# Second block's input projection: value units ahead of the gate units, chunk states beside the gate units, gate chains behind the states

## The chip, the cores and the metric

One NeuronCore of a Trainium2 chip runs the whole program. The metric is device time in microseconds of one execution; three runs of the kernel before gave 2759.41, 2761.75 and 2762.43 us, median 2761.75.

## The reference

Two transformer blocks on 512 tokens of width 1024, all in float32. The first has a SwiGLU, a mixer of 16 heads and another SwiGLU. The second puts 16 learned tokens in front (528 in all), normalises, and multiplies by one input matrix of 2000 columns. Its columns are, in this order: queries q and keys k of a gated linear attention (4 heads, 64 wide each), its values v (4 heads of 128 columns), its gate r (4 heads of 128), a 16-wide decay input, and the latents of a second attention (256 for queries, 128 for keys and values, 64 for the rotated key). What matters here, cut short:

```
z = u @ w_in
q, k, v, r, a_low, q_lat, kv_lat, k_rope = split(z)
b = cumsum(log_sigmoid(a_low @ w_a2 + b_a) / 16)   per chunk of 64 tokens
att = tril((q*exp(b)) @ (k*exp(-b)).T)             within a chunk
upd = (k*exp(b_last - b)).T @ v                    one per chunk
state = exp(b_last) * state + upd                  a scan over the chunks
o = att @ v + (q*exp(b)) @ state_before
y_gla = rmsnorm(o) * gain * silu(r)
y_mla = softmax attention over the latents, with rotated queries and keys
h = h + [y_gla, y_mla] @ w_out
```

After it comes a mixture of 64 experts (2 per token) and a last norm.

## The kernel before, in words

Each engine has its own program, written out in order by hand; semaphores join them. Nothing is planned by a scheduler, so an instruction runs when all ahead of it on its engine have been issued and its own waits are met.

Weights come through six SBUF slots of 2 MB. The SP queue issues the loads in a fixed order; before each it waits until the slot is free, a signal of TensorE. The input matrix of the second block comes as four items: item 3 (latents and decay input) in slot 2, item 0 (q and k) in slot 3, item 2 (gate) in slot 4, item 1 (values) in slot 5. The loads of those two slots that follow are the two halves of the output matrix, L619.

The projection is a list of units, `UNITS`, numbered in the order in which TensorE does them. Unit n writes PSUM bank 0 (even n) or 2 (odd n), and starts when the copy of unit n − 2 to SBUF is done (`unit`, L968). Each is 8 contraction steps with 512 columns. The gate units (U_GR, four of them, one per head) and the value units (U_GV: one for the 16 learned tokens and four for 128 tokens each) are at the end of the list. Copies are done by VectorE for the units in `ON_DVE`, which holds gate units 1 and 3 of four, and by ScalarE for the others.

TensorE's order from L1076: decay input and latents, keys, queries, the turned decayed keys (`turn_keys`), four gate units, then the value units with the chunk updates 0 to 6 between them. `chunk_update(n)` (L1024) writes banks 4 to 7 in turn; it waits for the copy of its value tile and, from n = 4 on, for the state n − 3. Then come the first score product (`gla_scores(0)`, bank 0, L1031), update 7, and the first two latent units (`mla_unit`, L1065 and L1067; the second one waits for the last state). Then, for each of four heads: the output product (`gla_out`, L1045 and L1048, which waits for the masked scores and, for head 0, for the last state), the next score product, a latent unit for keys (L1072), the sum of squares (`gla_sum`, L1054) and the next two latent units.

VectorE's order: copies and decay terms; for each pair of heads the gate chain: copy of the first unit of the pair, wait for ScalarE's exponential of minus the gate over both heads, add one (L1925), reciprocal over 1024 columns (L1926), product with the gate (L1927). It then does states 0 to 6 (`state`, four small instructions each, L1934), the first mask (`gla_mask(0)`, L1944), state 7, and for each head the rotation of the queries (`rope_queries`, L1961 to L1966), the next mask and the head's end (`gla_head`: reciprocal L1949, L1950, L1951).

ScalarE's order: copies; for each pair the copy of its second unit and the exponential over both (`gate_pair_exp`, L1483), then the copies of the five value units, then the copies and square roots of the heads' part. Its exponential of the second pair waits until the first pair's gate is done, since both use one buffer `gexp`.

All engines meet at the end of this stage (L486 is the helper of that meeting). Softmax attention over the latents, the output product, the router and the expert loop follow; the SP queue asks for the first expert's weights when the attention's last head is copied (`s_mo`).

Of the kernel before, what the change touches and what calls it, by code (L numbers as in the profile page):

```python
# [13 lines left out]
P = 128  # L14
# [36 lines left out]
GH = 4  # L51
# [81 lines left out]
def build(nc, a, out):  # L133
    ctx = ExitStack()
    with ctx:
# [290 lines left out]
        w_out2 = a["w_out_2"][0].rearrange("(f p) n -> p f n", p=P)  # L426
        ITEMS2 = [(0, 512), (512, 512), (1024, 512), (1536, 464)]

        ITEM_SLOT = {3: 2, 0: 3, 2: 4, 1: 5}

        def w2(n):
            return ring[ITEM_SLOT[n]][:, 0:KC * ITEMS2[n][1]].rearrange("p (k n) -> p k n", k=KC)
# [1 line left out]
        UNITS = [(3, 0, 16, True, aL[0:16, :]), (3, 16 + 2 * P, P, True, kv), (3, 16 + 3 * P, ROPE, True, kr[0:ROPE, :]),  # L434
                 (3, 16, P, False, ql[:, 0]), (3, 16 + P, P, False, ql[:, 1]),
                 (0, 2 * P, P, True, gk[:, 0]), (0, 3 * P, P, True, gk[:, 1]), (0, 0, P, False, gq[:, 0]), (0, P, P, False, gq[:, 1]),
                 (2, 0, P, False, gr[:, 0]), (2, P, P, False, gr[:, 1]), (2, 2 * P, P, False, gr[:, 2]), (2, 3 * P, P, False, gr[:, 3]),
                 (1, 0, META, None, gv[0:META, 0]), (1, 0, P, None, gv[:, 1]), (1, 0, P, None, gv[:, 2]),
                 (1, 0, P, None, gv[:, 3]), (1, 0, P, None, gv[:, 4])]
        U_AL, U_KV, U_KR, U_QL, U_GK, U_GQ, U_GR, U_GV = 0, 1, 2, 3, 5, 7, 9, 13  # L440
        ON_DVE = (U_KR, U_GK, U_GK + 1, U_GR, U_GR + 2)

        def unit_out(n):
# [86 lines left out]
        def _(sp):  # L530
# [68 lines left out]
                    .then_inc(filled[s], 16)  # L599
            u.take(0, 0)  # L600
            ffn(1)
            for n in (3, 0, 2, 1):
                c0, w = ITEMS2[n]
                slot_n = ITEM_SLOT[n]
                sp.wait_ge(freed[slot_n], u.take(slot_n, 1)[1])
                sp.dma_start(w2(n), w_in2[:, :, c0:c0 + w]).then_inc(filled[slot_n], 16)
                if n == 3:
                    sp.wait_ge(freed[1], u.take(1, 2)[1])
                    sp.dma_start(w_a2, a["gla_w_a2_2"][0]).then_inc(filled[1], 16)
                    sp.dma_start(w_qb, a["mla_w_qb_2"][0].rearrange("(k p) n -> p k n", p=P)).then_inc(filled[1], 16)  # L610
# [82 lines left out]
        def _(pe):  # L693
# [274 lines left out]
            def unit(n):  # L968
                it, c0, m, wide, _ = UNITS[n]
                if n == 0 or UNITS[n - 1][0] != it:  # L970
                    if n:
                        pe.drain().then_inc(freed[ITEM_SLOT[UNITS[n - 1][0]]], 1)
                    pe.wait_ge(filled[ITEM_SLOT[it]], u.take(ITEM_SLOT[it], 1)[0] + 16)
                if n >= 2:
                    pe.wait_ge(*unit_out(n - 2))
                b = 2 * (n % 2)
                for k in range(KC):
                    if n == 0:
                        pe.wait_ge(s_hn, KC * 3 + k + 1)
                    flags = dict(start=(k == 0), stop=(k == KC - 1))  # L980
                    if wide is None:
                        t = n - U_GV
                        last = mm(ps[0:m, b, :], hT[:, k, TILE0[t]:TILE0[t] + m], w2(it)[:, k, :], **flags)
                    elif wide:
                        for g in range(2):
                            last = mm(ps[0:m, b + g, 0:264], w2(it)[:, k, c0:c0 + m], hT[:, k, g * 264:(g + 1) * 264], **flags)
                    else:
                        last = mm(ps[0:m, b, :], w2(it)[:, k, c0:c0 + m], hT[:, k, META:TOK], **flags)
                last.then_inc(s_p2, 1)
# [95 lines left out]
            unit(U_GQ)  # L1085
            unit(U_GQ + 1)
            turn_keys()
            for h in range(GH):
                unit(U_GR + h)
            unit(U_GV)  # L1090
            unit(U_GV + 1)
            chunk_update(0)
# [4 lines left out]
            chunk_update(3)  # L1097
            chunk_update(4)
            unit(U_GV + 4)
            pe.drain().then_inc(freed[ITEM_SLOT[1]], 1)  # L1100
            chunk_update(5)
            chunk_update(6)
            pe.wait_ge(s_kd, 2)
            gla_scores(0)
            chunk_update(7)
            mla_unit(0)
            mla_unit(1)
            for h in range(GH):
# [201 lines left out]
        def _(act):  # L1310
# [197 lines left out]
            av(kdtok[:, 1:3, :], flat[:, 2304:2816].rearrange("p (t n) -> p t n", t=2), ACT.Copy)  # L1508
            av(kdtok[:, 3:5, :], flat[:, 2816:3328].rearrange("p (t n) -> p t n", t=2), ACT.Copy)
            av(kdtok[0:META, 0, :], ps[0:META, 4, 0:256], ACT.Copy).then_inc(s_ktc, 1)  # L1510
            for pair in range(2):
                unit_copy(U_GR + 2 * pair + 1)
                gate_pair_exp(pair)
            for t in range(5):
                unit_copy(U_GV + t)

            def mla_unit_copy(n):
                h, kind = n // 3, n % 3
# [104 lines left out]
        def _(dve):  # L1623
# [251 lines left out]
            def unit_copy(n):  # L1875
                dve.wait_ge(s_p2, n + 1)
                v.tensor_copy(unit_dst(n), unit_psum(n)).then_inc(s_p2c[0], 1)
# [41 lines left out]
            v.tensor_tensor(kd, kd, gk, ALU.mult).then_inc(s_kd, 1)  # L1919
            dve.wait_ge(*unit_out(U_GQ + 1))  # L1920
            v.tensor_tensor(gq, gq, eb[:, :, :], ALU.mult).then_inc(s_kd, 1)
            for pair in range(2):
                unit_copy(U_GR + 2 * pair)
                dve.wait_ge(s_gex, pair + 1)
                link(v.tensor_scalar(gexp, gexp, 1.0, None, ALU.add))  # L1925
                link(v.reciprocal(gexp, gexp))  # L1926
                v.tensor_tensor(gr[:, 2 * pair:2 * pair + 2, :], gr[:, 2 * pair:2 * pair + 2, :], gexp, ALU.mult).then_inc(s_gf, 1)  # L1927

            def state(n):
                dve.wait_ge(s_U, n + 1)  # L1930
                for p in range(2):
# [22 lines left out]
            def rope_queries(h):  # L1954
# [9 lines left out]
                                            op0=ALU.mult, op1=ALU.mult))  # L1964
                link(v.tensor_tensor(swap[0:ROPE, 0:SEQ], swap[0:ROPE, 0:SEQ], sin, ALU.mult))
                v.tensor_tensor(qr[:, h, :], qr[:, h, :], swap[0:ROPE, 0:SEQ], ALU.add).then_inc(s_mb, 1)  # L1966
            for n in range(N_CHUNK - 1):
                state(n)
            gla_mask(0)
            state(N_CHUNK - 1)  # L1970
            for h in range(GH):
                rope_queries(h)
                if h + 1 < GH:
# [276 lines left out]
```

## Time and profile before

| | |
|---|---|
| median of three runs | 2761.75 us |
| the profiled execution | 2760.66 us |
| its span, first to last instruction | 2758.8 us |
| TensorE busy | 2479.5 us, 90% |
| VectorE busy | 1050.5 us, 38% |
| ScalarE busy | 479.5 us, 17% |
| mean granted TensorE clock | 0.950 of full speed |
| input projection of the second block, gate and value units | about 1445 to 1514 us |
| end of the stage of the change | 1559.57 us |

PE is TensorE, PEld its weight load, DVE VectorE, ACT ScalarE, POOL GpSimd, SP the queue that issues loads. All times on an axis are microseconds from the start of the span. A bracket behind a row gives the idle time before it on its engine, and what ended that. A group that covers several instructions of one kind shows where the first began and how long until the last was done; matmuls are pipelined, so groups overlap by about 0.1 us. The granted clock is a share of full speed: 1.00 is 2.4 GHz and 0.50 is 1.2 GHz.

### The profile page before, as it was taken

Reading aid. Unit: us, or ns where it says so; the run is one execution under the profiler, and the core shown is the slowest. Engines: PE = TensorE matmul, PEld = TensorE weight load, DVE = VectorE, ACT = ScalarE, POOL = GpSimd, SP = SyncE. Lnnn points to the kernel's source line nnn. Section 1 sums busy time; section 2 is a strip of 40 time slices with the busy share of each in tenths; the row PEclk is TensorE's granted clock in tenths of the full one; section 3 lists DMA queues with packets and bytes.
Section 4 is the critical chain, followed back from the end, with each engine's and each line's share of the span. In section 5 each row is a group of like instructions: output and inputs, shape, how many; then the busy total and the mean of one; then the engine's idle time right before and its main releaser. Section 6 shows DMA issues by size and latency. Waiting matters only on the chain. (4 is left out here: it accounts for less than half of the span.)

```text
span 2758.8 us, 24417 instructions
## 1 busy us (share of the span) xinstructions
PE 2479.5 (90%) x8987; PEld 1140.9 (41%) x8987; DVE 1050.5 (38%) x1244; ACT 479.5 (17%) x751; POOL 177.8 (6%) x452
## 2 busy tenths in 40 slices
PE   8999999999898999999899998988888878888883
PEld 4444444466564444444354554323333323333231
DVE  3555640144563333320134634433333333333333
ACT  2000000156341100000121321111111111111111
POOL 0000000000000000000000000111111111111110
PEclk9999999999899999999999999998999999999896
DMA  7443744011201112412301022999999999999994
GB/s 278 148 147 131 211 133 109 24 46 47 84 1 61 61 61 91 113 32 79 136 12 54 8 107 115 374 417 417 415 412 405 414 412 406 402 412 413 403 416 157
DMA packets 182670, 563.06 MB, mean 204 GB/s; under 512 B 16732, under 2 KB 132716, under 8 KB 156384
## 3 DMA queue, kind: packets, MB, share of 16 engines
q1 hardware_dynamic: 172384, 554.10, 52.6%
q0 software_dynamic: 10240, 8.31, 1.0%
q8 instruction: 34, 0.56, 0.1%
q14 instruction: 12, 0.10, 0.0%
HBM read 566.66 MB, written 20.97 MB: 213 GB/s over the span
## 5 line engine op out<-in xcount | busy, mean ns | idle before, releaser
L1254 PE MATMUL ps<-slot,xT 128*64 128x512 f32 x2048 | 512.8, 658 | 155.2 <-DMA slot<-in_expert_w_up 149.0
L770 PE MATMUL ps<-hT,slot 128*128 128x512 f32 x1408 | 613.3, 596 | 13.0 <-ACT hT L1349 7.2
L770 PEld LDWEIGHTS ps<-hT,slot 128*128 128x128 f32 x1408 | 267.2, 191 | 350.6 <-issue 347.4
L1254 PEld LDWEIGHTS ps<-slot,xT 128*64 128x64 f32 x2048 | 154.9, 151 | 509.9 <-issue 308.4
L799 PE MATMUL ps<-big,slot 128*128 128x512 f32 x704 | 306.0, 594 | 3.3 <-issue 2.9
L2137 DVE COPY hT<-ps 128x256 f32<-128x256 f32 x64 | 27.2, 425 | 621.0 <-PE ps L1262 621.0
L1273 PE MATMUL ps<-slot,hT 128*64 128x512 f32 x1024 | 238.2, 608 | 1.2 <-DVE hT L2137 1.2
L2128 DVE RECIPROCAL xT<-xT 64x512 f32<-64x512 f32 x64 | 214.1, 3345 | 2.2
L799 PEld LDWEIGHTS ps<-big,slot 128*128 128x128 f32 x704 | 132.4, 190 | 176.1 <-issue 176.1
L1710 DVE RECIPROCAL eb<-eb 128x512 f32<-128x512 f32 x44 | 147.5, 3353 | 1.5
L1708 DVE TENSOR_SCALAR eb<-eb 128x512 f32<-128x512 f32 x44 | 18.8, 427 | 330.6 <-ACT eb L1359 330.6
L1583 ACT ACTIVATE xT<-ps 64x512 f32<-64x512 f32 x64 | 37.9, 592 | 587.5 <-PE ps L1254 587.5
L1273 PEld LDWEIGHTS ps<-slot,hT 128*64 128x64 f32 x1024 | 69.4, 138 | 118.1 <-issue 113.9
L1589 ACT ACTIVATE hT<-ps 64x512 f32<-64x512 f32 x128 | 75.9, 593 | 205.8 <-PE ps L1273 205.1
L1734 DVE SCALAR_TENSOR_TENSOR xT<-ps,small,xT 128x512 f32<-128x512 f32 x16 | 12.0, 751 | 250.7 <-PE ps L799 250.5
L821 PE MATMUL ps<-hT,slot 128*128 128x512 f32 x240 | 105.8, 596 | 0.0
L2188 POOL MEMSET spare<- 1x4 f32 x1 | 0.1, 92 | 1619.8 <-DVEq L486 1619.8
L1359 ACT ACTIVATE eb<-ps 128x512 f32<-128x512 f32 x44 | 26.3, 597 | 418.6 <-PE ps L770 418.5
L1336 ACT ACTIVATE tmp<-xT 128x512 f32<-128x512 f32 (+1 forms) x32 | 20.2, 633 | 334.2 <-DVE xT L1734 298.5
L821 PEld LDWEIGHTS ps<-hT,slot 128*128 128x128 f32 x240 | 44.8, 190 | 55.1 <-issue 55.1
L827 PE MATMUL ps<-slot,hT 128*128 128x128 f32 x512 | 60.4, 280 | 6.9 <-DVE big L1798 6.9
L1236 PE MATMUL ps<-cst,xT 64*128 64x64 f32 x496 | 64.9, 272 | 0.0
(353 smaller groups left out, 2272.6 us busy)
## 6 DMA issues: line engine op xcount, KB each, us to landing
slot<-in_expert_w_gate SPq DMA_DIRECT2D x64, 2048.0 KB, 19.3
slot<-in_expert_w_up SPq DMA_DIRECT2D x64, 2048.0 KB, 22.3
slot<-in_expert_w_down SPq DMA_DIRECT2D x64, 2048.0 KB
slot<-in_w_mod SPq DMA_DIRECT2D x18, 2048.0 KB, 15.8
slot<-in_w_gate SPq DMA_DIRECT2D x22, 1024.0 KB, 5.5
slot<-in_w_up SPq DMA_DIRECT2D x22, 1024.0 KB, 8.0
slot<-in_w_down SPq DMA_DIRECT2D x16, 1408.0 KB, 8.0
slot<-in_w_in SPq DMA_DIRECT2D x24, 512.0 KB, 5.8
```

The source lines that it names most:

```text
L770: last = mm(ps[:, 2 * j + g, :], w[:, g, k, j * P:(j + 1) * P], hT[:, k, META:TOK], start=(k == 0), stop=(k == KC - 1))
L799: last = mm(ps[:, down_bank(d), :], w[:, f, :], aT[:, f, :], start=(f == 0), stop=(f == FC - 1))
L821: last = mm(ps[:, bank, :], pair_w[p][:, k, m, :], hT[:, k, META:TOK], start=(k == 0), stop=(k == KC - 1))
L827: last = mm(ps[:, bank, t * P:(t + 1) * P], hT[:, k, META + t * P:META + (t + 1) * P], pair_w[p][:, k, 2, :], start=(k == 0), stop=(k == K ...
L1236: last = nc.tensor.transpose(ps[:, 4 + j, k * CAP:(k + 1) * CAP], xs[j].rearrange("p (m k) -> p k m", k=KC)[:, k, :], ident[0:CAP, 0:CAP])
L1254: last = mm(ps[g * CAP:(g + 1) * CAP, j, :], xsT[j][:, k, :], w[g][:, k, :], start=(k == 0), stop=(k == KC - 1))
L1273: last = mm(ps[g * CAP:(g + 1) * CAP, 2 + j, :], hid[j][:, c, :], w[:, c, g * 512:(g + 1) * 512], start=(c == 0), stop=(c == 3))
L1583: av(sg[j], ps[0:CAP, j, :], ACT.Exp, scale=-1.0).then_inc(s_eg, 1)
L1589: last = av(ys[j][:, g * 512:(g + 1) * 512], ps[g * CAP:(g + 1) * CAP, 2 + j, :], ACT.Copy)
L1710: v.reciprocal(eb[:, j, :], eb[:, j, :]).then_inc(s_vec, 1)
L2128: v.reciprocal(sg[j], sg[j]).then_inc(s_vec, 1)
L2137: v.tensor_copy(hid[j].rearrange("p c s -> p (c s)"), ps[:, 6 + j, 0:4 * CAP]).then_inc(s_hd, 1)
```

## The change

The unit list has the value units at numbers 9 to 13 and the gate units at 14 to 17. Items 1 and 2 change slots (1 in slot 4, 2 in slot 5), and the SP queue loads item 1 ahead of item 2. TensorE does the value units and updates 0 to 6 right after the turned keys, then gate unit 1, update 7, gate units 2 to 4, the drain that frees slot 5, and then waits additionally for the copy of gate unit 3 before the first score product, which writes the same PSUM bank. ScalarE copies the value units first, then the gate pairs with their exponentials. VectorE does all eight states, then both gate chains, then the first mask.

```diff
--- before.py
+++ after.py
@@ -426,7 +426,7 @@
         w_out2 = a["w_out_2"][0].rearrange("(f p) n -> p f n", p=P)
         ITEMS2 = [(0, 512), (512, 512), (1024, 512), (1536, 464)]
 
-        ITEM_SLOT = {3: 2, 0: 3, 2: 4, 1: 5}
+        ITEM_SLOT = {3: 2, 0: 3, 1: 4, 2: 5}
 
         def w2(n):
             return ring[ITEM_SLOT[n]][:, 0:KC * ITEMS2[n][1]].rearrange("p (k n) -> p k n", k=KC)
@@ -434,10 +434,10 @@
         UNITS = [(3, 0, 16, True, aL[0:16, :]), (3, 16 + 2 * P, P, True, kv), (3, 16 + 3 * P, ROPE, True, kr[0:ROPE, :]),
                  (3, 16, P, False, ql[:, 0]), (3, 16 + P, P, False, ql[:, 1]),
                  (0, 2 * P, P, True, gk[:, 0]), (0, 3 * P, P, True, gk[:, 1]), (0, 0, P, False, gq[:, 0]), (0, P, P, False, gq[:, 1]),
-                 (2, 0, P, False, gr[:, 0]), (2, P, P, False, gr[:, 1]), (2, 2 * P, P, False, gr[:, 2]), (2, 3 * P, P, False, gr[:, 3]),
                  (1, 0, META, None, gv[0:META, 0]), (1, 0, P, None, gv[:, 1]), (1, 0, P, None, gv[:, 2]),
-                 (1, 0, P, None, gv[:, 3]), (1, 0, P, None, gv[:, 4])]
-        U_AL, U_KV, U_KR, U_QL, U_GK, U_GQ, U_GR, U_GV = 0, 1, 2, 3, 5, 7, 9, 13
+                 (1, 0, P, None, gv[:, 3]), (1, 0, P, None, gv[:, 4]),
+                 (2, 0, P, False, gr[:, 0]), (2, P, P, False, gr[:, 1]), (2, 2 * P, P, False, gr[:, 2]), (2, 3 * P, P, False, gr[:, 3])]
+        U_AL, U_KV, U_KR, U_QL, U_GK, U_GQ, U_GR, U_GV = 0, 1, 2, 3, 5, 7, 14, 9
         ON_DVE = (U_KR, U_GK, U_GK + 1, U_GR, U_GR + 2)
 
         def unit_out(n):
@@ -599,7 +599,7 @@
                     .then_inc(filled[s], 16)
             u.take(0, 0)
             ffn(1)
-            for n in (3, 0, 2, 1):
+            for n in (3, 0, 1, 2):
                 c0, w = ITEMS2[n]
                 slot_n = ITEM_SLOT[n]
                 sp.wait_ge(freed[slot_n], u.take(slot_n, 1)[1])
@@ -1085,8 +1085,6 @@
             unit(U_GQ)
             unit(U_GQ + 1)
             turn_keys()
-            for h in range(GH):
-                unit(U_GR + h)
             unit(U_GV)
             unit(U_GV + 1)
             chunk_update(0)
@@ -1097,12 +1095,16 @@
             chunk_update(3)
             chunk_update(4)
             unit(U_GV + 4)
-            pe.drain().then_inc(freed[ITEM_SLOT[1]], 1)
             chunk_update(5)
             chunk_update(6)
+            unit(U_GR)
+            chunk_update(7)
+            for h in range(1, GH):
+                unit(U_GR + h)
+            pe.drain().then_inc(freed[ITEM_SLOT[2]], 1)
             pe.wait_ge(s_kd, 2)
+            pe.wait_ge(*unit_out(U_GR + 2))
             gla_scores(0)
-            chunk_update(7)
             mla_unit(0)
             mla_unit(1)
             for h in range(GH):
@@ -1508,11 +1510,11 @@
             av(kdtok[:, 1:3, :], flat[:, 2304:2816].rearrange("p (t n) -> p t n", t=2), ACT.Copy)
             av(kdtok[:, 3:5, :], flat[:, 2816:3328].rearrange("p (t n) -> p t n", t=2), ACT.Copy)
             av(kdtok[0:META, 0, :], ps[0:META, 4, 0:256], ACT.Copy).then_inc(s_ktc, 1)
+            for t in range(5):
+                unit_copy(U_GV + t)
             for pair in range(2):
                 unit_copy(U_GR + 2 * pair + 1)
                 gate_pair_exp(pair)
-            for t in range(5):
-                unit_copy(U_GV + t)
 
             def mla_unit_copy(n):
                 h, kind = n // 3, n % 3
@@ -1919,13 +1921,6 @@
             v.tensor_tensor(kd, kd, gk, ALU.mult).then_inc(s_kd, 1)
             dve.wait_ge(*unit_out(U_GQ + 1))
             v.tensor_tensor(gq, gq, eb[:, :, :], ALU.mult).then_inc(s_kd, 1)
-            for pair in range(2):
-                unit_copy(U_GR + 2 * pair)
-                dve.wait_ge(s_gex, pair + 1)
-                link(v.tensor_scalar(gexp, gexp, 1.0, None, ALU.add))
-                link(v.reciprocal(gexp, gexp))
-                v.tensor_tensor(gr[:, 2 * pair:2 * pair + 2, :], gr[:, 2 * pair:2 * pair + 2, :], gexp, ALU.mult).then_inc(s_gf, 1)
-
             def state(n):
                 dve.wait_ge(s_U, n + 1)
                 for p in range(2):
@@ -1964,10 +1959,15 @@
                                             op0=ALU.mult, op1=ALU.mult))
                 link(v.tensor_tensor(swap[0:ROPE, 0:SEQ], swap[0:ROPE, 0:SEQ], sin, ALU.mult))
                 v.tensor_tensor(qr[:, h, :], qr[:, h, :], swap[0:ROPE, 0:SEQ], ALU.add).then_inc(s_mb, 1)
-            for n in range(N_CHUNK - 1):
+            for n in range(N_CHUNK):
                 state(n)
+            for pair in range(2):
+                unit_copy(U_GR + 2 * pair)
+                dve.wait_ge(s_gex, pair + 1)
+                link(v.tensor_scalar(gexp, gexp, 1.0, None, ALU.add))
+                link(v.reciprocal(gexp, gexp))
+                v.tensor_tensor(gr[:, 2 * pair:2 * pair + 2, :], gr[:, 2 * pair:2 * pair + 2, :], gexp, ALU.mult).then_inc(s_gf, 1)
             gla_mask(0)
-            state(N_CHUNK - 1)
             for h in range(GH):
                 rope_queries(h)
                 if h + 1 < GH:
```

## Rows read from the trace of the kernel before

**Rows 1.** The page: busy time of each engine over the span.
```profile
PE 2479.5 (90%) x8987; PEld 1140.9 (41%) x8987; DVE 1050.5 (38%) x1244; ACT 479.5 (17%) x751; POOL 177.8 (6%) x452
```

**Rows 2.** Stretches: window, length, busy per engine, granted TensorE clock, DMA share, GB/s.
```profile
1445.00:1560.00 115.00, 110.55 (x374) 53.44 (x374) 65.37 (x77) 23.09 (x35) 0.00 (x0) 1.00 0.12 40
...
1750.00:2710.00 960.00, 809.12 (x3702) 303.69 (x3698) 338.87 (x310) 146.49 (x247) 170.12 (x429) 0.93 0.99 407
```

**Rows 3.** TensorE in order of time: start, us, line, operation, count, [idle before <- releaser].
```profile
1445.30 27.70 PE L988 MATMUL ps<-hT,slot 128*128 128x512 f32 x64 [0.26 <-issue]
...
1512.94 1.05 PE L1031 MATMUL ps<-big,slot 64*128 64x128 f32 x8
1513.83 1.03 PE L1024 MATMUL ps<-big 64*128 64x256 f32 x4
1514.79 1.98 PE L1065 MATMUL ps<-big,slot 128*128 128x512 f32 x4
1518.22 1.93 PE L1067 MATMUL ps<-big,slot 128*64 128x512 f32 x4 [1.45 <-DVE slot L1934]
1520.08 1.16 PE L1045 MATMUL ps<-eb,big 128*128 128x128 f32 x8
```

**Rows 4.** ScalarE in order of time, around the second gate pair.
```profile
1459.98 1.28 ACT L1483 ACT_TABLE_LOAD   x1
...
1473.04 0.60 ACT L1476 ACTIVATE big<-ps 128x512 f32<-128x512 f32 x1 [10.71 <-PE ps L988]
1473.72 1.06 ACT L1483 ACTIVATE slot<-big 128x1024 f32<-128x1024 f32 x1
```

**Rows 5.** VectorE in order of time: copy, second gate pair, states, first mask, first head.
```profile
1470.82 0.68 DVE L1877 COPY big<-ps 128x512 f32<-128x512 f32 x1
1474.81 0.70 DVE L1925 TENSOR_SCALAR slot<-slot 128x1024 f32<-128x1024 f32 x1 [3.30 <-ACT slot L1483]
1475.54 6.55 DVE L1926 RECIPROCAL slot<-slot 128x1024 f32<-128x1024 f32 x1
1482.12 1.22 DVE L1927 TENSOR_TENSOR big<-big,slot 128x1024 f32<-128x1024 f32 x1
...
1513.21 2.89 DVE L1934 SCALAR_TENSOR_TENSOR slot<-slot,glst,ps 64x128 f32<-64x128 f32 x8 [5.54 <-PE ps L1024]
1516.14 0.69 DVE L1944 TENSOR_TENSOR eb<-ps,cst 128x512 f32<-128x512 f32 x1
...
1527.49 3.35 DVE L1949 RECIPROCAL tmp<-tmp 128x512 f32<-128x512 f32 x1 [3.04 <-ACT tmp L1533]
```

**Rows 6.** Stretches chosen around pauses of TensorE: granted clock in the third last column.
```profile
527.38:531.58 4.20, 4.20 (x5) 1.81 (x6) 3.55 (x9) 4.20 (x7) 0.00 (x0) 0.50 0.00 0
...
732.98:736.38 3.40, 3.40 (x16) 3.40 (x17) 2.78 (x7) 2.51 (x6) 0.00 (x0) 0.50 0.00 0
890.53:896.36 5.83, 0.00 (x0) 0.03 (x1) 5.04 (x4) 1.65 (x3) 0.00 (x0) 0.75 0.00 0
896.36:900.22 3.86, 3.86 (x5) 1.80 (x6) 3.22 (x6) 3.86 (x6) 0.00 (x0) 0.50 0.00 0
1366.20:1372.22 6.02, 0.00 (x1) 0.03 (x1) 5.08 (x4) 1.73 (x4) 0.00 (x0) 0.64 1.05 397
1372.22:1378.05 5.83, 5.83 (x14) 2.00 (x15) 3.41 (x6) 4.24 (x7) 0.00 (x0) 0.50 0.74 268
1516.72:1518.22 1.50, 0.05 (x2) 0.00 (x1) 1.40 (x5) 0.60 (x1) 0.00 (x0) 1.00 0.99 410
1562.42:1572.34 9.92, 8.60 (x22) 4.50 (x21) 3.24 (x11) 3.22 (x11) 0.00 (x0) 0.50 0.00 1
```

**Rows 7.** The SP queue in order of time: issues of loads.
```profile
1473.08 39.11 SPq L619 DMA_DIRECT2D slot<-in_w_out  x2
...
1620.58 0.43 SPq L626 DMA_DIRECT2D slot<-in_expert_w_gate  x1
```

**Rows 8.** The page, DMA issues: count, KB each, median us from issue to landing.
```profile
slot<-in_w_out SPq DMA_DIRECT2D x2, 2048.0 KB, 8.1
```

## The prediction

> **What bounds the kernel now.** I read the page's totals first, then the span cut into stretches, then the order of time on TensorE, VectorE and ScalarE in the stage that changes. TensorE is busy for 2479.5 us, 90% of the span [rows 1], but that average mixes stages. From 1750 to 2710 us the DMA share is 0.99 and TensorE idles 151 us: the expert loop is bound by its weight stream, of fixed length, and begins when the work ahead of it is done. In the stage of the change, 1445 to 1560 us, the DMA share is 0.12, TensorE is busy for 110.55 of 115 us and VectorE for 65.37 [rows 2]. So here TensorE's order in time is the clock, and VectorE has slack, but only where its chains lie beside TensorE work. The four gate units run without a gap for 27.70 us from 1445.30; the state updates of the value part end at 1514.79, where the first latent unit starts; the second latent unit waits 1.45 us (for the last state, which VectorE reaches after the first mask); the first head's output product starts at 1520.08 [rows 3]. A later start of that product is a later start of everything behind it: the SP queue's first expert weights go out at 1620.58, behind a wait on the attention that follows [rows 7], so no prefetch absorbs a slip.
>
> **The change part by part.**
>
> *Swapping slots, loads and unit numbers.* Items 1 and 2 are both 2 MB, slots 4 and 5 are waited for in the same order, and the projection at 1445.30 finds its weights there with no DMA wait [rows 3]: 0 for the first item in its new order, and the second item has 40 us more. The output weights of slot 4 now start when the value units end (about 1484 us instead of 1473.08), and those of slot 5 after the last gate unit (about 1514; now 1512). They are used after 1620, so at least 100 us cover both; if that cover were gone, the price would be one such load from issue to landing, 8.1 us [rows 8]. On the SP queue nothing is behind them but the loads that wait for the attention [rows 7]. I take 0, bounds 0 to +0.3.
>
> *TensorE's own work.* No matmul is added or removed; there are three changes of weight item with a drain before and after. From 1445.30 to 1514.79 are 69.49 us, in which the first score product takes 1513.83 − 1512.94 = 0.89 [rows 3]. That product is now after all units, so gate unit 4 ends at X = 1445.30 + 69.49 − 0.89 = 1513.90. Waits inside: update 7 wants state 4, and the copy of value tile 4, both long done since gate unit 1 (6.9 us, a quarter of 27.70) stands in between; gate unit 3 wants VectorE's copy of gate unit 1, which comes right behind the last state. Counted back from X: four gate units and update 7 take 28.0 us, so gate unit 1 runs from 1485.9 to 1492.8, update 7 is done at 1493.1, a state is half of 2.89 us and the copy 0.68 [rows 5], so that copy is done near 1495.3, ahead of the end of gate unit 2 (the start of unit 3) at 1500.0. 0 for all of it, bounds −0.3 to +0.5.
>
> *First gate pair.* Its chain from the end of gate unit 2 is the one worked out below for the second pair, 10.34 us, and a table load of 1.28 us [rows 4]: done at 1511.6, and VectorE's copy of gate unit 3 (0.68, [rows 5]) at 1512.3. The first score product waits for that copy, because both use PSUM bank 0. It is ready 1.6 us ahead of X: cost 0. The cover is gate unit 4's own 6.9 us; without it the wait would be 5 us.
>
> *Second gate pair: the term that decides.* It now starts when gate unit 4 is done, and the first mask stands behind it on VectorE. The trace has the same chain: gate unit 4 ended at 1473.00, ScalarE's copy began at 1473.04 and its exponential at 1473.72 [rows 4], VectorE's add at 1474.81, reciprocal 6.55, product from 1482.12 for 1.22, done at 1483.34 [rows 3, 5]. So 1483.34 − 1473.00 = 10.34 us from the end of the unit. Then the mask, 0.69, and two hand-overs of 0.03 (the exponential ended at 1474.78 and VectorE went on at 1474.81 [rows 4, 5]). The first output product starts at 1513.90 + 10.34 + 0.69 + 0.06 = 1524.99. TensorE has beside it the score product (0.89) and the two latent units (1518.22 to 1520.08 is 1.86 for the second, and 1.98 less an overlap, say 1.9, for the first): 4.7 us, so it idles from about 1518.6 to 1525.0, 6.4 us. The 1.45 us wait for the last state is gone: that state is ready near 1494.6. Net at this point: 1524.99 − 1520.08 = +4.9 us. Queued behind the mask on VectorE are the query rotation, mask 2 and the first head's chain; all of them follow the mask or TensorE's product as before (rotation 3.5 us, mask 2 behind score product 2), and VectorE's wait of about 3 us before the reciprocal at 1527.49 [rows 5] is a wait for TensorE and ScalarE, not slack that could take this up. Bounds: +4.0 (the add overlaps the exponential's tail more, the first latent unit is later) to +5.5.
>
> *The clock.* TensorE's granted clock fell during idle stretches of this size: 5.83 us idle from 890.53 has a mean of 0.75, 6.02 us idle from 1366.20 a mean of 0.64, while 1.50 us around the present wait kept 1.00. After work came back the grant stayed at 0.50, the lower level of 1.2 GHz, for 3.86 and 5.83 us; after two shorter pauses for 4.20 and 3.40 [rows 6]. The mean is 4.32 us; at half rate 2.16 us of work is lost. The work there is the first output product, score product 2 and the first square sum, on which the reciprocal at 1527.49 waits and from which on VectorE runs almost without a pause to the stage's end; the loss is on the path. Bounds 0 (no fall) and 2.9 (half of 5.83), widened by what a low stretch at 1562.42 of 9.92 us shows [rows 6]: up to 5.0.
>
> The Trainium skill, "TensorE: Matmul & The Clock Gate", section "Part 1: The HAM clock gate", says that half rate is the default, that only activity lifts it, and that the monitor's window is free-running, so that the moment of a transition varies from run to run. By that rule the stall of this change is paid twice (+4.9 and then the slow work, together +7.1); if one only counted idle time, it would be +4.9. The trace agrees: full-rate idle pauses are followed by 0.50, and the low time after them varies, 3.40 to 5.83 us [rows 6].
>
> *The later stretches* move as a whole. The low stretch from 1562.42 begins in a phase change with small pauses; moved by some microseconds it may be shorter or longer. I take no change, bounds −3.3 (9.92 shrinks to 3.40, half of the difference) and +2.
>
> **Sum.** 0 + 0 + 4.91 + 2.16 = +7.1 us. The profiled execution took 2760.66 us with a span of 2758.8; its forecast is 2767.8. It stands 1.09 us under the median of 2761.75, which I move by the same: 2768.85, so 2768.8.
>
> **The rivals.**
> (A) The forecast, +7.1: 2766.5 to 2771. 0.58.
> (B) The stall comes but the slow clock costs nothing, since it falls late or its loss lies beside VectorE: +4.9, 2766.7. For it: the three-microsecond wait before 1527.49. Against: that wait is for the very products that are slowed, and a stall of 6.4 us is longer than each of those in which the grant fell. 0.17.
> (C) The second chain is out of the way by the end of the latent units, and only the lost wait counts: −1.45, 2760.3, not slower. Its place is the mask at VectorE; it decides if the chain from the end of gate unit 4 to the mask takes under 4.7 us, the TensorE work beside it. For it: the wait of 1.45 us is real and goes. Against: the one reciprocal takes 6.55 us [rows 5]. 0.05.
> (D) The low clock lasts as at 1562.42 or the later low stretch lengthens: 4.9 + 5.0 = +9.9 and up, 2771.7 to 2774. For it: that stretch had TensorE busy 8.60 of 9.92 us and stayed low. Against: there the work was small products behind softmax; here TensorE has 3.6 us of dense work, then more. 0.14.
> (E) The stall comes and the stretch at 1562.42 shrinks by luck: 7.1 − 3.3 = +3.8, 2765.6. 0.06.
>
> **Chances.** A measurement of this kernel tells about 0.2% (5.5 us) from no change, so slower is above 2767.3. A gives 0.85 of its chance to that, B a quarter, E a tenth, D all: 0.68. Faster by over 5.5 us needs C together with a luckier clock later: 0.03. Within: 0.29. The range from 2765.0 to 2772.5 takes in A, B, E and half of D.
>
> **What would show it.** In the profile after: gate unit 4 ends near 1514; one TensorE idle of 6 to 6.5 us before the first output product, released by the VectorE mask; no wait at the second latent unit; second reciprocal of 6.55 us lying in that idle time; a granted clock of 0.50 for 3 to 6 us after it; the stage's end later by about 7 us and everything behind it by the same. It would be wrong if the mask did not follow the second gate chain, if the clock held 1.00 through the stall (then B), or if the later stage returned what was lost (E).

## The result: slower, by more than the range allowed

The changed kernel took 2776.0 us in the median of seven runs (2772.08 to 2778.86), the kernel before 2762.43 (2759.41 to 2772.87): ratio 1.0037, interval [1.0021, 1.0054]. The forecast was 2768.8 with a range to 2772.5. The direction was right, the size was not.

The profiled execution has a span of 2777.0 us instead of 2758.8. First TensorE in order of time, with the rows that answer to [rows 3]:

```profile
1446.06 14.09 PE L983 MATMUL ps<-slot,hT 128*16 128x512 f32 x32 [0.26 <-issue]
...
1485.91 7.10 PE L988 MATMUL ps<-hT,slot 128*128 128x512 f32 x16 [0.31 <-issue]
1492.95 1.13 PE L1024 MATMUL ps<-big 64*128 64x256 f32 x4
1494.01 20.87 PE L988 MATMUL ps<-hT,slot 128*128 128x512 f32 x48
1515.13 1.13 PE L1031 MATMUL ps<-big,slot 64*128 64x128 f32 x8 [0.26 <-issue]
1516.19 1.98 PE L1065 MATMUL ps<-big,slot 128*128 128x512 f32 x4
1518.11 1.93 PE L1067 MATMUL ps<-big,slot 128*64 128x512 f32 x4
1525.87 2.08 PE L1045 MATMUL ps<-eb,big 128*128 128x128 f32 x8 [5.84 <-DVE eb L1939]
1527.88 3.03 PE L1048 MATMUL ps<-big,slot 64*128 64x64 f32 x13
...
1537.81 1.93 PE L1067 MATMUL ps<-big,slot 128*64 128x512 f32 x4
```

The wait of 1.45 us before the second latent unit is gone; one of 5.84 us stands before the first output product, released by the first mask. Behind it the same product takes 2.08 us where it took 1.16 [rows 3]. ScalarE's copy and exponential for the second gate pair, which answer to [rows 4]:

```profile
1514.91 0.60 ACT L1478 ACTIVATE big<-ps 128x512 f32<-128x512 f32 x1 [10.71 <-PE ps L988]
1515.59 1.06 ACT L1485 ACTIVATE slot<-big 128x1024 f32<-128x1024 f32 x1
```

VectorE at the same place, which answers to [rows 5]:

```profile
1512.69 0.68 DVE L1879 COPY big<-ps 128x512 f32<-128x512 f32 x1
1516.68 0.69 DVE L1967 TENSOR_SCALAR slot<-slot 128x1024 f32<-128x1024 f32 x1 [3.30 <-ACT slot L1485]
1517.41 6.55 DVE L1968 RECIPROCAL slot<-slot 128x1024 f32<-128x1024 f32 x1
1523.99 1.22 DVE L1969 TENSOR_TENSOR big<-big,slot 128x1024 f32<-128x1024 f32 x1
1525.13 0.68 DVE L1939 TENSOR_TENSOR eb<-ps,cst 128x512 f32<-128x512 f32 x1
...
1537.31 3.35 DVE L1944 RECIPROCAL tmp<-tmp 128x512 f32<-128x512 f32 x1 [4.01 <-ACT tmp L1535]
```

The chain that lay under the value units now ends at the mask. Stretches of the changed kernel, with the granted clock in the third last column: the idle time, the work behind it, the whole stage of softmax attention (from the meeting of the engines to the issue of the first expert weights), and its low part:

```profile
1520.00:1525.87 5.87, 0.04 (x1) 0.00 (x0) 5.80 (x4) 0.00 (x0) 0.00 (x0) 0.69 0.33 135
1525.87:1535.20 9.33, 9.33 (x37) 8.03 (x38) 4.08 (x6) 1.13 (x2) 0.00 (x0) 0.50 0.00 0
1569.38:1637.87 68.49, 64.61 (x296) 43.69 (x296) 24.55 (x80) 19.96 (x65) 0.09 (x1) 0.80 0.00 1
1573.60:1593.90 20.30, 20.07 (x60) 13.09 (x60) 5.26 (x18) 4.46 (x16) 0.00 (x0) 0.50 0.00 0
```

The same attention stage in the kernel before:

```profile
1559.57:1620.58 61.01, 57.20 (x296) 38.14 (x296) 24.67 (x80) 19.93 (x65) 0.09 (x1) 0.91 0.00 1
```

So the 18.2 us between the two spans are made of: 0.8 that this execution was late before the stage began (keys turned at 1445.79 instead of 1445.03); 5.0 from there to the first output product (80.08 instead of 75.05); 4.0 from there to the stage's end (43.51 instead of 39.49), where no instruction was added and the clock is what differs (x4b_kept_busy_6 below shows that it is the cause); 7.5 in the attention (68.49 instead of 61.01), the same instructions with a mean clock of 0.80 instead of 0.91; 0.9 in the rest. The forecast put the attention's part at nothing.

### The profile page after: what moved, and what is told of

It is laid out like the page before. It is cut to its first block and busy times, and to the rows that moved or that the text cites. A ratio compares the mean times of both kernels' runs of the same rounds, so it can differ in the third digit from the quotient of the medians.

```text
span 2777.0 us, 24418 instructions
## 1 busy us (share of the span) xinstructions
PE 2494.8 (90%) x8987; PEld 1152.4 (41%) x8987; DVE 1050.1 (38%) x1244; ACT 479.0 (17%) x751; POOL 177.0 (6%) x452
```

## The experiments

In the table, A is the time from the turned keys to the first output product, B from there to the meeting of the engines, C from there to the first expert weights, all from each kernel's profile; then the mean and the ends of its timed runs in us. Two groups of times are given apart where a gap of over 2 us has three runs or more on each side; the widest is taken.

```
kernel                      A      B      C      runs  mean    times
before                      75.05  39.49  61.01  148   2766.5  76 in 2756.7-2765.4, 72 in 2769.7-2775.7
before_again                75.04  39.49  69.37   12   2769.9  3 in 2762.1-2764.2, 9 in 2771.0-2773.3
after                       80.08  43.51  68.49    7   2775.1  3 in 2772.1-2773.0, 4 in 2776.0-2778.9
after_again                 80.07  43.51  68.50   12   2776.1  6 in 2771.4-2772.8, 6 in 2776.1-2791.8
x1_swap_only                75.05  39.48  69.34   10   2767.8  4 in 2757.1-2763.3, 6 in 2770.4-2776.0
x2_mask_first               74.20  43.83  60.96   10   2770.2  5 in 2763.6-2768.2, 5 in 2774.4-2776.4
x3_no_second_reciprocal     74.18  39.48  68.48    1   2772.1
x4_kept_busy (13)           85.47  39.37  69.47   10   2777.6  4 in 2770.4-2772.9, 6 in 2780.2-2783.5
x4b_kept_busy_6             80.09  39.48  80.10   12   2781.1  4 in 2773.5-2776.9, 8 in 2782.5-2785.7
x13_later_2                 76.86  39.38  66.51   12   2770.4  8 in 2766.1-2770.9, 4 in 2774.6-2777.7
x13_later_4                 78.58  39.38  69.39   12   2772.7  4 in 2763.0-2766.8, 8 in 2774.6-2778.9
x13_later_6                 80.29  39.38  66.52   12   2774.6  8 in 2769.7-2774.6, 4 in 2779.0-2781.5
with matmuls added at two pauses around the attention's start:
x7_attention_busy           75.05  40.24  58.13   12   2761.3  2755.9-2766.8
x8_after_both_busy          80.08  40.25  57.32   12   2765.2  2762.7-2768.5
x9_after_attention_busy     80.09  44.27  61.47   12   2770.1  2766.9-2772.2
x5b_extra_reciprocal        79.91  44.28  57.31   12   2768.3  2767.1-2771.4
x10_mask_first_busy         74.17  44.62  59.33   12   2766.9  5 in 2761.9-2765.5, 7 in 2767.9-2770.9
x14_state_first_busy        74.44  40.25  57.32   11   2758.8  7 in 2755.4-2758.1, 4 in 2761.1-2763.8
```

The first row's times are all runs of the kernel before, taken beside the others. They were taken in several lots, and the mean of before differs between them: 2767.4 beside after_again, x4b and x7, 2766.2 beside x8, x9, x5b and x10, 2765.7 beside x13 and x14. So a difference of about 1.5 us between kernels of different lots is not a finding.

**Only the slots.**
```diff
-        ITEM_SLOT = {3: 2, 0: 3, 2: 4, 1: 5}
+        ITEM_SLOT = {3: 2, 0: 3, 1: 4, 2: 5}
-            for n in (3, 0, 2, 1):
+            for n in (3, 0, 1, 2):
```


> The kernel before with only the slots of items 1 and 2 exchanged and item 1 loaded ahead of item 2; the order on the engines stays. Theory (the stall of TensorE behind the second gate chain and the low clock after it make the loss): no difference, within 0.2% of before, and the first output product starts 1520 us into the span, as before. Rival (the loads or their slots cost time): some of the 10 to 14 us show here.

Measured: ratio 1.0005 [0.9982, 1.0028]; A and B as before, both groups of times as before. (The expected 1520 us into the span came at 1522.60, since the keys were turned 2.5 us later.) The swap costs nothing that shows in A, B or the groups; the total alone would leave room for −5 to +8 us.

**The mask ahead of the second chain.**
```diff
             for pair in range(2):
                 unit_copy(U_GR + 2 * pair)
+                if pair:
+                    gla_mask(0)
                 dve.wait_ge(s_gex, pair + 1)
...
-            gla_mask(0)
```


> The changed kernel with VectorE's first mask between the copy of gate unit 3 and the add of the second gate pair; nothing else moves. Theory: the first output product starts right behind the second latent unit, 5.8 us earlier than in the changed kernel (1520.0 instead of 1525.9), and TensorE has no idle of 5.84 us there. The second chain (about 8.6 us on VectorE) then delays the query rotation, so a pause of up to 3.4 us shows ahead of the third latent unit; the stage ends 5 to 8 us earlier than in the changed kernel and 1 to 5 us later than before. Rival (the order of the units itself costs): the stage ends as late as in the changed kernel.

Its TensorE in order of time:

```profile
1517.81 1.93 PE L1067 MATMUL ps<-big,slot 128*64 128x512 f32 x4
1519.67 1.16 PE L1045 MATMUL ps<-eb,big 128*128 128x128 f32 x8
...
1528.73 3.65 PE L1065 MATMUL ps<-big,slot 128*128 128x512 f32 x4 [3.48 <-DVE slot L1961]
```

The stall is gone from its place and A is 0.85 us shorter than before, since the wait of 1.45 us for the state is gone and part of it is lost again in smaller pauses. VectorE owes the 8.5 us all the same: the pause turns up as 3.48 us ahead of the third latent unit, and the granted clock is 0.50 there too (the third latent unit takes 3.65 us, 1.88 in the changed kernel). A + B is 5.6 us less than in the changed kernel and 3.5 more than before.

**The second reciprocal left out.**
```diff
-                link(v.reciprocal(gexp, gexp))
+                if pair == 0:
+                    link(v.reciprocal(gexp, gexp))
```


> The changed kernel with the reciprocal of the second gate pair left out (the gate of heads 2 and 3 is multiplied by 1 + exp instead of divided by it), so that the choice of experts behind it may differ; only the stage is read. Theory: the chain is 6.6 us shorter and ends at about the time when the second latent unit does, so TensorE does not idle before the first output product (under 0.5 us), the granted clock stays 1.00 there, and from 1446 to the end of the stage it takes about 10 us less than in the changed kernel (5.0 of stall and 4 of low clock), that is, 0.5 to 1.5 us less than before. Rival (clock lost for another reason): at most 6.6 us less, with the low clock still there.

This kernel leaves out the reciprocal, so only the stage is read, from one profile: A 74.18, B 39.48, no pause, clock 1.00 in the stage. A + B is 9.9 us less than in the changed kernel and 0.9 less than before. 6.55 us of one VectorE instruction are worth 9.9 us here. Without that chain the new order would be better by the wait it removes.

**TensorE kept at work in the stall.**
```diff
+            for _ in range(13):        # 6 in x4b_kept_busy_6
+                mm(ps[:, 3, :], ident, xT[:, 0, META:TOK], start=True, stop=True)
             for h in range(GH):
                 gla_out(h)
```


> The changed kernel with 13 additional matmuls of 128x128 by 128x512 into an idle PSUM bank on TensorE between the second latent unit and the first output product, 5.6 us of work at full rate in an idle time of 5.84 us. Theory (stall, then a low clock): the output product starts at the same time as in the changed kernel (1525.9), the granted clock stays 1.00, and the stage ends 4 us earlier than in the changed kernel, 5 us later than before. Rival (the 4 us are queueing on VectorE and ScalarE, not the clock): the stage ends as in the changed kernel.

I had the length of such a matmul wrong by two: 13 took 11.4 us and moved the product by 5.4 (A 85.47). B is 39.37 all the same, 4.1 less than in the changed kernel.

> As x4_kept_busy, with 6 additional matmuls instead of 13: one takes 0.87 us (two passes of 0.43), so 13 were 11.4 us and moved the output product by 5.5 us; 6 are 5.2 us and fit the idle time of 5.84. Theory: the first output product starts 80.1 us after the turned keys, as in the changed kernel, the granted clock stays 1.00 to the stage's end, which comes 39.4 us later (43.5 in the changed kernel, 39.5 before): 4 us earlier than in the changed kernel's first profile, and a mean 5 us above the mean of before. Rival (the slow clock costs nothing beside VectorE): as the changed kernel.

With six the product starts where it starts in the changed kernel, and B is 39.48: the 4.0 us of B are the slow clock's and not a queue on VectorE or ScalarE. The stage and the attention behind it:

```profile
1526.13:1565.61 39.48, 37.25 (x178) 22.00 (x178) 34.59 (x35) 13.59 (x21) 0.00 (x0) 1.00 0.00 1
1565.61:1645.71 80.10, 76.22 (x296) 51.16 (x296) 24.37 (x80) 20.20 (x65) 0.09 (x1) 0.68 0.00 1
```

The stage is as expected and the total is not: the mean is 5.1 us above after_again instead of below it, because the attention took 80.10 us at a mean clock of 0.68. Four microseconds won in one stage were more than given back in the next (11.6 in the profiles). That turned the question to the attention.

**Both kernels again, for their spread.** No edit.

> The kernel before, unchanged, for the spread of its times and one more profile. Theory (the attention stage behind the change has two lengths, 61 and about 69 us from the stage's end to the first expert weights, by how long the granted clock stays at 0.50 from its first microseconds on): two groups of times, near 2760 and 2772, with nothing between 2764 and 2770; the profile shows the stage itself as before (39.5 us from the first output product to the stage's end) and the attention at 61 or at 69 us. Rival (the 7.5 us in the attention were caused by the change): one group near 2761.

The kernel before in its other form:

```profile
1561.49:1630.86 69.37, 65.69 (x296) 44.06 (x296) 24.46 (x80) 20.04 (x65) 0.09 (x1) 0.78 0.00 1
```

The long attention is the kernel's own: half of its 148 runs lie in the upper group, 11.3 us above the lower in the mean (2772.3 and 2761.0). The two profiled executions, one from each group, differ by 10.8 us in the span: 8.4 in the attention, 1.9 ahead of the keys.

> The changed kernel, unchanged, for the spread of its times and one more profile. Theory: every run carries the stall of 5.0 us and 1.7 to 5 us of low clock behind it, on top of one or the other length of the attention: times between 2766 and 2783, mean 8 to 10 us above the mean of before. In the profile the first output product starts 80.1 us after the keys are turned (75.05 before). Rival (the change always puts the attention in its long form): one group near 2776.

A and B repeat to 0.01 us. The mean of its 19 runs is 2775.7, 9.2 above the mean of before, as expected; one run, of 2791.8, lies outside the expected times. The rival of one group near 2776 fell: there is a second one near 2772.

**Matmuls at two pauses around the attention's start.**
```diff
+            for _ in range(2):
+                mm(ps[:, 5, :], ident, xT[:, 0, META:TOK], start=True, stop=True)
             phase_end(pe, 14)
...
             scores(0)
             scores(1)
+            for _ in range(2):
+                mm(ps[:, 7, :], ident, xT[:, 0, META:TOK], start=True, stop=True)
```


> The kernel before with additional matmuls of 128x128 by 128x512 into idle PSUM banks: two ahead of the meeting of the engines at the stage's end (pause of 1.04 us) and two behind the first two score products of the attention (pause of 1.3 us), 0.87 us each. Theory (the clock falls at 1562 because of these pauses, and the short form is a lucky recovery): the clock holds 1.00 through the attention in most runs, from the stage's end to the first expert weights it takes 55 to 58 us instead of 61 or 69, and the times form one group near 2755 to 2758. Rival (the small products of the attention do not hold the clock whatever stands ahead): two groups as before, 1 us later.

```profile
1562.00:1620.13 58.13, 55.64 (x300) 37.54 (x300) 24.73 (x80) 19.76 (x65) 0.09 (x1) 0.98 0.00 1
```

Four matmuls of useless work, 3.5 us of TensorE, and the two groups are gone: ratio 0.9975 [0.9959, 0.9991] to the kernel before, though the spread was not as narrow, nor the time as low, as expected. The clock holds 1.00 until the attention's last 2.6 us. With this the change can be priced with less of the attention's lottery. In the next four the same lines are added to other kernels. These four belong to another lot than x7; against its own runs of before each mean stands at −6.0 us (x7), +3.9 (x9), −0.9 (x8), +2.2 (x5b) and +0.8 (x10), each with a standard error of 1 to 1.5 us.

> The changed kernel with the four additional matmuls of x7_attention_busy, which hold the clock at 1.00 in the attention, so that what the change costs in its own stage is read without the attention's two lengths. Theory: one group of times, 7 to 10 us above x7_attention_busy (5.0 of stall, 2 to 4.7 of low clock behind it), near 2769 to 2771; attention of 58 us; the stage from the turned keys on 9 us longer. Rival (the change also lengthens the attention by itself): 12 us or more above x7, or again two groups.

8.8 us above x7 in the mean: A + B + C is 12.4 us more in the profiles, 5.0 in A, 4.0 in B, 3.3 in C, where the clock stood at 0.50 for 3.4 us at the start and 7.1 at the end. (The two executions differ by 9.1 us only, since x9's keys were turned 2.9 us earlier.)

> x9_after_attention_busy with the 6 additional matmuls of x4b_kept_busy_6 in the stall as well. Theory: the stall of 5.0 us alone remains, so one group 5 us above x7_attention_busy and 2 to 4.7 us below x9_after_attention_busy, near 2766. Rival (matmuls in the stall put the attention behind it into a longer form, as the profile of x4b_kept_busy_6 with its 80 us might be read): no gain over x9.

3.9 above x7 (5.1, each against its own lot) and 4.9 below x9: with the clock at 1.00 through both stages only the stall is left.

```diff
-            gla_mask(0)
             state(N_CHUNK - 1)
+            link(v.reciprocal(gexp, gexp))
+            gla_mask(0)
```


> x7_attention_busy (order of the kernel before) with one additional reciprocal of 128x1024 on an unused buffer ahead of VectorE's first mask, behind the last state. Theory (it is only the time at which the mask is reached that counts, not the order of the units or the slots): the first output product starts 80 us after the turned keys, as in the changed kernel, with an idle of about 5 us and a low clock behind it; the time is that of x9_after_attention_busy within 1.5 us. Rival (the order of units and loads costs): it stays 3 us or more below x9.

The old order of units, loads and slots, with one reciprocal more on VectorE and the last state ahead of the mask:

```profile
1519.75 1.93 PE L1067 MATMUL ps<-big,slot 128*64 128x512 f32 x4 [0.85 <-DVE slot L1938]
1527.07 2.08 PE L1045 MATMUL ps<-eb,big 128*128 128x128 f32 x8 [5.38 <-DVE eb L1948]
```

A 79.91, B 44.28: the change's stall and slow stretch rebuilt in the old order by one more VectorE instruction ahead of the mask. It is 7.0 us above x7 and 1.8 below x9, a little more than the 1.5 allowed.

> x9_after_attention_busy with the first mask ahead of the second gate chain, as in x2_mask_first. Theory: the first output product starts 74.2 us after the turned keys, 0.85 us earlier than before, as in x2; but the chain of 8.5 us then stands ahead of the query rotation, and from the product to the stage's end it is 43.8 us instead of 39.5, so the time is 3.5 us above x7_attention_busy (less one more us if the clock does not fall at the pause of the third latent unit). Rival (with the stall gone the new order wins 1.4 us): 1 us below x7.

5.6 us above x7 where 3.5 were expected: in the profiles A + B is 3.5 more and C 1.2; the rest is not placed. Not below x7, so the rival fell. The times of x10 and of x14 below part again, by gaps of 2.5 and 3.0 us, so the four matmuls do not take away every cause of spread.

**The attention moved in time, nothing else changed.** The matmuls of x4 put into the kernel before, 2, 4 or 6 of them, where there is no idle time.

> The kernel before with 2 additional matmuls (1.73 us) between the second latent unit and the first output product, no idle time and no low clock in the stage. Theory (the moment at which the attention begins, within the run, decides how long its low clock lasts): groups of times that are not those of before moved by 1.7 us (2762.5 and 2774.2), but further up, by some 5 us or more in part of the runs. Rival (the stall or the order of the change lengthens the attention): 2762.5 and 2774.2.

> The same with 4 matmuls (3.47 us). Theory: as for the kernel whose stage ended 3.5 us later for another reason (x2_mask_first, groups near 2764.6 and 2775.2), two groups as before, moved by 3.5: 2764.3 and 2775.9. Rival (no dependence on the moment): the same here, so that only the runs with 2 and 6 tell them apart.

> The same with 6 matmuls (5.20 us). Theory: as x4b_kept_busy_6, whose stage ended 5.0 us later (2775.2 and 2784.2), 8 us above what 5.2 us alone would give; attention of 69 to 80 us in the profile. Rival (the change's order or its chain at the end lengthens the attention): 2766.0 and 2777.6.

The attention of x13_later_2, with a third length:

```profile
1560.17:1626.68 66.51, 62.62 (x296) 42.05 (x296) 24.57 (x80) 19.96 (x65) 0.09 (x1) 0.85 0.00 1
```

With four the two groups are those of before moved by 3.5 us. With two and with six the lower group is 4 and 6 us higher than a mere shift would put it (near 2766.7 instead of 2762.5, near 2772 instead of 2766.0), and the profiles show 66.5 us. So the moment at which the attention begins does bear on how long its clock stays low, without any stall or new order. But x13_later_6 did not repeat the 2775 and 2784 of x4b_kept_busy_6; with the same delay x4b lies 6.5 us higher in the mean.

The profiles show where the two part. In each of the twelve without matmuls at the attention's pauses the clock falls to 0.50 once, within its first 5 us, and how long it stays there goes with where in the stage it fell; in ten of them it is low again at the stage's end. The first low stretch in before, before_again, x13_later_6 and x4b_kept_busy_6:

```profile
1562.41:1572.65 10.24, 8.92 (x23) 4.67 (x23) 3.24 (x11) 3.23 (x11) 0.00 (x0) 0.50 0.00 1
1563.17:1587.07 23.90, 22.70 (x66) 14.20 (x66) 6.43 (x23) 6.62 (x19) 0.00 (x0) 0.50 0.00 0
1569.97:1590.45 20.48, 20.48 (x62) 13.32 (x62) 5.01 (x17) 4.29 (x14) 0.00 (x0) 0.50 0.00 0
1570.27:1614.64 44.37, 44.37 (x135) 29.09 (x133) 10.85 (x36) 9.14 (x30) 0.00 (x0) 0.50 0.00 1
```

All twelve (times in us; the last two columns are the low time at the stage's end, and C):

```
clock falls after   stays low   kernels                              at the end   C
1.6 to 1.7          23.9        before_again, x1, x4, x13_later_4    6.2 to 6.4   69.3 to 69.5
2.8                 10.2        before, x2                           0.2          61.0
3.7 to 4.0          20.5        after, after_again, x3               6.5 to 6.8   68.5
4.5                 20.5        x13_later_2, x13_later_6             0            66.5
4.7                 44.4        x4b_kept_busy_6                      7.2          80.1
```

The profile of before_again is from the upper group of before (first row) and that of before from the lower (second row). Of the 7.5 us between before and after, 5.5 go with the longer first stretch (66.51 in x13_later_2, which has it and no low end) and the other 2.0 with the low end. And x4b's fall at 4.66 us instead of 4.52 goes with 44 us low instead of 20. That is a regularity of twelve profiles and not an experiment; what sets the moment of the fall, and what the upper group of x13_later_6 looks like, is open.

**The last state ahead of the mask**, in the old order, with the four matmuls of x7.
```diff
-            gla_mask(0)
             state(N_CHUNK - 1)
+            gla_mask(0)
```


> x7_attention_busy with the last state ahead of the first mask on VectorE (order of the units as before): the second latent unit waits 0.7 us less. Theory: 0 to 0.8 us below x7_attention_busy, not to be told from it in the times; the trace shows the wait before the second latent unit at 0.7 us instead of 1.45. Rival (the mask, now later, holds the first output product): no gain in the trace either.

```profile
1516.19 1.93 PE L1067 MATMUL ps<-big,slot 128*64 128x512 f32 x4 [0.84 <-DVE slot L1938]
```

The wait is 0.84 us instead of 1.45. The ratio to before is 0.9967 [0.9952, 0.9983]. Its mean is 2.5 us below x7's, but the two belong to different lots; each against its own, it is 0.8 us, near the 0.6 that the trace shows in A, and too little to be told from nothing by the times. This version and x7 beat both kernels. The better half of the idea behind the change (the state ready before it is wanted) is had in the trace without moving a unit.

## Why the prediction was wrong, point by point

- *Slots and loads, 0*: right (x1_swap_only).
- *TensorE's own work, gate unit 4 at 1513.90*: it ended at 1494.01 + 20.87 = 1514.88, of which 0.76 is the late start: 1514.12. The copy of gate unit 3 was done at 1513.37, in time.
- *The second gate chain, 10.34 us*: 1525.21 − 1514.88 = 10.33. The product started at 1525.87, without the late start 1525.11; forecast 1524.99. Idle 5.84, forecast 6.4, since the pause ahead of the score product, that product and the latent units filled 0.5 more. The term +4.91 measured 5.03. x3 and x5b show that this chain makes it.
- *The clock behind the stall, +2.16*: mis-sized. The grant stayed at 0.50 for 9.33 us of work instead of 4.32, and cost 4.02. The value was the mean of four stretches of [rows 6]; what came is longer than all four, and near the fifth, the 9.92 us that I had kept as the upper bound. That the loss is on the path was right: B falls back to 39.48 when the clock is held (x4b). The Trainium skill, "TensorE: Matmul & The Clock Gate", section "Part 1: The HAM clock gate", says that half rate is the default, that activity lifts it, and that the moment of a transition varies from run to run. The runs agree: the stall was paid twice (+5.03 and then +4.02, where idle time alone would have given 5.03), and in two profiles of the same kernel the clock fell 2.8 and 1.7 us after the attention's start.
- *The later stretches, "I take no change, bounds −3.3 and +2"*: the step that failed. The attention took 7.48 us more in the profile. With the stall and the clock behind it as measured, and nothing here, the forecast would have been 2770.8, inside its range. The row of the 9.92 us at 1562.42 was in my hands, as luck that could end sooner; I did not ask what it would cost if it went on longer. In the kernel before it does so too: 8.4 us in the profile of before_again, and half of the runs lie in the upper group.
- *The base*: the profile and the three runs of before were all from its lower group. Against the mean of 148 runs, 2766.5, the change costs 9.2 us; the two medians of seven differ by 13.6. Rival D named the mechanism at 0.14 and gave 2771.7 to 2774. Both of its halves came, the long low clock behind the stall and the longer later stretch, and the time lies above even its upper end.

What part of the 9.2 us is what: 5.0 of stall, shown by A in after, after_again, x9, and in x8 and x4b, where six extra matmuls fill it (x5b: 4.9); 4.0 of low clock behind it, shown by B in after, after_again, x9 and x5b (x9 against x8: 4.9 in the mean). That is 9.0, so in the mean 0.2 us is left for the attention, to some 2.4 us either way. Its 7.5 us made the profile and the first median look worse, but no run shows that the change makes the attention longer on average: the kernel before takes the long form in half of its own runs.

## What to carry to other kernels

A VectorE chain that hides under TensorE work is free only there: ask, for each chain that a reordering puts last, what stands behind it on its engine and which TensorE instruction waits for that. Price a TensorE stall with the slow work behind it, here 5.0 + 4.0 us. And where a later stage already runs at a low clock for a while in the one profile at hand, take that stretch as something that may come out otherwise in the next execution: look at a second profile before a change is judged by a median of few runs.

## What was not expected of the hardware

The granted clock alone, with the same 296 matmuls, gives the attention stage 57.3, 61.0, 66.5, 68.5, 69.4 or 80.1 us, at mean clocks of 1.00, 0.91, 0.85, 0.80, 0.78 and 0.68 (the first with two matmuls more, four records). In the changed kernel the clock stood at 0.50 for 20.30 us in which TensorE was busy for 20.07, and in x4b_kept_busy_6 for 44.37 us in which it was busy throughout. Four extra matmuls, 3.5 us, at two pauses kept it at 1.00 through the attention's start in five of the six profiles that have them, and low there for 3.4 us in the sixth. Useless work at the right place is worth about 5 us on the mean of this kernel.
